# Scores of the latent attention as three rounded products instead of fp32 ones, high parts made by ScalarE and low parts by GpSimd

## The chip, the cores and the metric

One Trainium2 chip, one of its cores. The metric is the device time of one launch in microseconds. The kernel before was run three times: median 1334.41 us, from 1334.18 to 1334.98. The engines are called PE (TensorE), ACT (ScalarE), DVE (VectorE), POOL (GpSimd) and SP (SyncE); PEld is PE's weight load.

## The reference

A trunk of two layers runs over two requests of 256 tokens, 1024 channels, in float32. The even layer has, beside Mamba-2 heads (SSD), eight heads of multi-head latent attention (MLA); its part is

```
q = einsum('bsr,rf->bsf', rmsnorm(q_a, q_norm_w), w_qb)      # per head 128 "nope" + 64 "rope" columns
c_kv = rmsnorm(kv_a[..., :128], kv_norm_w)
q_rope, k_rope = apply_rope(q[..., 128:]), apply_rope(kv_a[..., 128:])
q_lat = einsum('bshd,chd->bshc', q_nope, w_uk)
sc = einsum('bqhc,bkc->bhqk', q_lat, c_kv) + einsum('bqhr,bkr->bhqk', q_rope, k_rope)
pr = softmax(sc * (128 + 64) ** -0.5)
o = (pr @ c_kv) @ w_uv
```

The concatenation of the SSD output and o goes through w_out, a norm and the residual; then come a convolutional FFN, a layer of gated linear attention (GLA) and another FFN. The scores `sc`, of 128 + 64 contracted rows per head, are what the change is about.

## The kernel before, in words

Everything is kept transposed: a tile has 128 channels as partitions and T = 512 columns, 2 requests of 256 tokens. The program has one instruction list for each engine, written out by hand, with semaphores between them; every engine works through its list in order. A weight block is loaded by SP (`load`, L294), rounded by ACT into `whi` (`hi`, L306) and the rest is taken by POOL into `wlo` (`lo`, L312, L316); `three` (L329 to L335) then makes a product of three rounded (fp32r) ones, whi x high, whi x low and wlo x high, without the product of the two low parts. Nearly all of PE's time is L333, L334 and L335. `his` and `los` (L319, L324) split the blocks that are due at a point. A slot for a block is free again when the products on it have incremented `mm_block`, on which SP waits.

The attention stage runs from about 198 to 283 us of the span, for 8 heads in 4 pairs; i is the pair, u the head in it, n = 2i + u the head. In `pe_mla` (L1425) a pair's queries (`queries`, L1432), keys (`keys`, L1442), values by token (`by_token`, L1455) and rope part (`rope`, L1472) are rounded products of weights and of the normed latents. ACT copies them out of PSUM (`copy`, L1570, to qh, kh, vp), DVE multiplies the rope product with cosines and sines into qre (`rope`, L1643), two 64-row halves for each head. `kre` (L1404), the rotated key part shared by all heads, is the sum of two parts. These are float32 tiles, and the scores (`scores`, L1491) are float32 products, which the profile shows as two instructions each (x2):

```
first = nc.tensor.matmul(o, qh[u][:, q], kh[u][:, keys_of], start=True, stop=False)      # L1502
last = nc.tensor.matmul(o, qre[u][:, q], kre[:, keys_of], start=False, stop=True)        # L1505
```

for 2 requests and 2 blocks of 128 queries against 256 keys. DVE then takes the maxima (`top`, L1657) and scales them (L1660), ACT takes the exponentials (`soft`, L1591) in four parts, DVE normalises (`norm`, L1666 and L1670), PE transposes (`turn`, L1519), ACT and DVE each copy a half into probT (`turned`, L1601 and L1678), PE multiplies with the values (`values`, L1532), and ACT and DVE make the high and low parts of the output, co_hi and co_lo (`outs`, L1605 and L1682).

PE's order in the stage: the parts of pair 0; then for each head n: scores(n), turn(n-1), parts of the next pair (queries and keys of its first head on even n, rope, queries and keys of its second head on odd n), values(n-1), by_token on even n. by_token(1) stands in turn 1. scores(n) waits for the copies, for qre and for the exponentials of head n-1, which free its PSUM banks.

ACT's order: copies of pair 0 around the square of the last SSD chunk (`act_ssd_square`, L1229) and one weight split, then for each n: its half of probT of n-1, soft(n), two copies of the next pair, rounded SSD chunks (`act_ssd_high`, L1267), the high part of the output of n-1, two value copies on even n, weight splits on even n. Two square roots with a table load stand in turn 0.

DVE's order for each n: top(n), its half of probT of n-1, on odd n the rope parts of the next pair with a product on zbuf between (`dve_ssd_norm`, L1262), norm(n), the low part of the output of n-1, low parts of SSD chunks (`dve_ssd_low`, L1272), two reciprocals of 128 columns in turns 1 to 4 (L1206).

POOL's list has the sum of squares of the SSD chunks (L1141), the last of which waits for ACT's last square, and then in this stage only weight splits (`pool_mla`, L1711). Behind the stage `pe_out` (L389) multiplies with w_out, the first product beside the last values and turn; the chunks of xw_hi and xw_lo, co_hi and co_lo are its operands.

Pieces of SBUF that are free in this stage: the last chunk of co_lo (chunk 7), chunks 6 and 7 of co_hi, xw_hi and xw_lo are written only in its last turns.

## Time and profile before

| what | value |
|---|---|
| median of 3 runs | 1334.41 us |
| the profiled execution | 1333.35 us |
| its span in the profile | 1331.5 us |
| PE busy | 1312.0 us (99%) |
| DVE busy | 772.5 us (58%) |
| ACT busy | 642.2 us (48%) |
| POOL busy | 620.4 us (47%) |
| mean granted clock of PE | 0.998 |

The profile is of one execution; times in its rows are microseconds from the start of its span. The time of the execution is 1.85 us longer than the span. In a timeline a row is: start, duration, engine, line, operation, output tile <- inputs, shapes, count, and in brackets the idle time of the engine before it with what ended it. Rows with x2 or more merge neighbours. A matmul's duration goes over into the next one's; the distance of starts is what it takes of PE.

### The profile page before, as it was taken

Reading aid. Unit: us, or ns where it says so; the run is one execution under the profiler, and the core shown is the slowest. Engines: PE = TensorE matmul, PEld = TensorE weight load, DVE = VectorE, ACT = ScalarE, POOL = GpSimd, SP = SyncE. Lnnn points to the kernel's source line nnn. Section 1 sums busy time; section 2 is a strip of 40 time slices with the busy share of each in tenths; the row PEclk is TensorE's granted clock in tenths of the full one; section 3 lists DMA queues with packets and bytes.
Section 4 is the critical chain, followed back from the end, with each engine's and each line's share of the span. In section 5 each row is a group of like instructions: output and inputs, shape, how many; then the busy total and the mean of one; then the engine's idle time right before and its main releaser. Section 6 shows DMA issues by size and latency. Waiting matters only on the chain.

```text
span 1331.5 us, 16312 instructions
## 1 busy us (share of the span) xinstructions
PE 1312.0 (99%) x6566; PEld 1110.9 (83%) x6566; DVE 772.5 (58%) x846; ACT 642.2 (48%) x1033; POOL 620.4 (47%) x294
## 2 busy tenths in 40 slices
PE   7999999999999999999999999999999999999997
PEld 6878878888898888888889988888998888888887
DVE  5857386840079998885001863546379988882002
ACT  6654787653355544444223486654555444443221
POOL 3344561245524554445454354654534554445551
PEclk9999999999999999999999999999999999999999
DMA  6342111123323333333332323311223333333331
GB/s 207 95 116 83 51 37 41 64 80 95 90 85 96 97 102 101 95 91 88 103 98 84 122 64 95 96 50 68 89 96 95 97 103 100 96 89 90 98 88 64
DMA packets 41451, 119.77 MB, mean 90 GB/s; under 512 B 4384, under 2 KB 12960, under 8 KB 41376
## 3 DMA queue, kind: packets, MB, share of 16 engines
q1 hardware_dynamic: 40160, 116.34, 28.3%
q10 hardware_dynamic: 1216, 2.38, 0.6%
q8 instruction: 52, 0.85, 0.3%
q14 instruction: 23, 0.19, 0.0%
HBM read 116.35 MB, written 2.23 MB: 89 GB/s over the span
## 4 chain that ended last, share of the span: by engine, by line
PE 93%; DVE 4%; ACT 1%; issue 1%; DMA 0%; ACTq 0%; DVEq 0%
PE bank L333 27%; PE bank L334 26%; PE bank L335 26%; PE bank L1771 1%; PE bank L1770 1%; PE bank L1769 1%; PE bank L2009 1%; PE bank L1502 1%; PE bank L1505 1%; PE bank L1322 1%; PE bank L384 1%; PE bank L1991 1%; PE bank L1289 1%; PE bank L1532 1%; DVE sqacc L660 1%
## 5 line engine op out<-in xcount | busy, mean ns | idle before, releaser
L316 POOL TENSOR_TENSOR wlo<-raw,whi 128x1024 fp32r<-128x1024 f32 (+2 forms) x215 | 528.6, 2472 | 630.7 <-ACT whi L310 630.6
L333 PE MATMUL bank<-xw_hi,whi 128*128 128x512 f32 (+1 forms) x1280 | 477.4, 373 | 8.6 <-DVE xw_lo L643 8.1
L335 PE MATMUL bank<-xw_hi,wlo 128*128 128x512 f32 (+1 forms) x1280 | 473.3, 370 | 0.0
L334 PE MATMUL bank<-xw_lo,whi 128*128 128x512 f32 (+1 forms) x1280 | 473.3, 370 | 0.0
L310 ACT ACTIVATE whi<-raw 128x1024 fp32r<-128x1024 f32 (+2 forms) x217 | 221.5, 1025 | 205.9 <-DMA raw<-in_fout 112.0
L333 PEld LDWEIGHTS bank<-xw_hi,whi 128*128 128x128 f32 x1280 | 242.0, 189 | 50.2 <-issue 8.9
L335 PEld LDWEIGHTS bank<-xw_hi,wlo 128*128 128x128 f32 x1280 | 241.9, 189 | 41.1
L334 PEld LDWEIGHTS bank<-xw_lo,whi 128*128 128x128 f32 x1280 | 242.0, 189 | 39.9 <-issue 0.2
L593 DVE RECIPROCAL small<-small 128x2 f32<-128x2 f32 x8 | 1.3, 166 | 315.1 <-ACT small L518 313.8
L712 DVE SCALAR_TENSOR_TENSOR cbuf<-ubuf,par,cbuf 128x510 f32<-128x510 f32 x100 | 168.8, 1688 | 3.5
L708 DVE SCALAR_TENSOR_TENSOR cbuf<-ubuf,par,cbuf 128x510 f32<-128x510 f32 x100 | 155.9, 1559 | 4.7 <-ACT cbuf L841 4.1
L333 PE MATMUL bank<-g_hi,whi 128*128 128x512 f32 (+1 forms) x396 | 145.3, 367 | 0.2
L335 PE MATMUL bank<-g_hi,wlo 128*128 128x512 f32 (+1 forms) x396 | 144.7, 365 | 0.0
L334 PE MATMUL bank<-g_lo,whi 128*128 128x512 f32 (+1 forms) x396 | 144.7, 365 | 0.0
L717 DVE TENSOR_TENSOR ubuf<-bank,rstd 128x512 f32<-128x512 f32 x116 | 78.0, 686 | 100.5 <-PE bank L335 91.1
L753 ACT ACTIVATE g_hi<-cbuf 128x512 fp32r<-128x512 f32 x44 | 27.8, 632 | 197.3 <-DVE cbuf L779 197.3
L333 PEld LDWEIGHTS bank<-g_hi,whi 128*128 128x128 f32 x396 | 74.7, 189 | 13.1 <-DVE g_lo L761 1.0
L334 PEld LDWEIGHTS bank<-g_lo,whi 128*128 128x128 f32 x396 | 74.7, 189 | 12.1
L335 PEld LDWEIGHTS bank<-g_hi,wlo 128*128 128x128 f32 x396 | 74.7, 189 | 11.9
L742 ACT ACTIVATE cbuf<-ubuf,par 128x512 f32<-128x512 f32 x88 | 69.9, 813 | 29.9 <-DVE ubuf L717 29.9
L779 DVE TENSOR_TENSOR cbuf<-cbuf 128x512 f32<-128x512 f32 x44 | 36.7, 834 | 1.5
L572 POOL TENSOR_TENSOR sqacc<-sqacc,cbuf 128x512 f32<-128x512 f32 x23 | 29.7, 1291 | 15.9 <-ACT cbuf L493 15.6
(275 smaller groups left out, 1435.5 us busy)
## 6 DMA issues: line engine op xcount, KB each, us to landing
raw<-in_fin SPq DMA_DIRECT2D x88, 512.0 KB, 3.6
raw<-in_fout SPq DMA_DIRECT2D x32, 448.0 KB, 3.3
raw<-in_gin SPq DMA_DIRECT2D x25, 512.0 KB, 3.6
raw<-in_hin SPq DMA_DIRECT2D x24, 512.0 KB, 3.6
raw<-in_hout SPq DMA_DIRECT2D x16, 512.0 KB, 3.7
raw<-in_fout SPq DMA_DIRECT2D x16, 512.0 KB, 3.6
raw<-in_gout SPq DMA_DIRECT2D x8, 512.0 KB, 3.7
xres<-in_x SPq DMA_DIRECT2D x8, 256.0 KB, 5.8
```

Source lines behind the costliest of these rows:

```text
L310: nc.scalar.activation(whi[s][:, 0:n], raw[s][:, 0:n], ACT.Copy).then_inc(w_hi, 1)
L316: engine.tensor_tensor(wlo[s][:, 0:n], raw[s][:, 0:n], whi[s][:, 0:n].bitcast(F32), ALU.subtract).then_inc(w_lo, 1)
L333: first = nc.tensor.matmul(out_ap, wh, ah, start=start, stop=False)
L334: nc.tensor.matmul(out_ap, wh, al, start=False, stop=False)
L335: return first, nc.tensor.matmul(out_ap, wl, ah, start=False, stop=stop)
L572: nc.gpsimd.tensor_tensor(sqacc[:], sqacc[:], cbuf[c % 2][:], ALU.add).then_inc(sem("out_acc"), 1)
L708: nc.vector.scalar_tensor_tensor(out=req(dst[:])[:, :, 1:SEQ], in0=req(src[:])[:, :, 0:SEQ - 1], scalar=prm(w, of), in1=req(dst[:])[:, :, ...
L712: nc.vector.scalar_tensor_tensor(out=req(dst[:])[:, :, 0:SEQ - 1], in0=req(src[:])[:, :, 1:SEQ], scalar=prm(w, of + 2 * n), in1=req(dst[:] ...
L717: return nc.vector.tensor_tensor(out_ap, src[:], rstd[:], ALU.mult)
L742: nc.scalar.activation(cbuf[u][:], ubuf[u][:], ACT.Identity, bias=prm(f"fb{l}", u * FF + t), scale=prm(f"fw{l}", 2 * FF + u * FF + t)).the ...
L753: nc.scalar.activation(ck(g_hi, t), cbuf[3][:], ACT.Copy).then_inc(sem("fin_hi"), 1)
L779: nc.vector.tensor_tensor(cbuf[3][:], cbuf[2][:], cbuf[1][:], ALU.mult).then_inc(sem("fin_prod"), 1)
```

## The change

The tiles qh, kh, qre and kre stay as float32 tiles; a rounded tile of the same size (qh_lo and so on) lies at the same address, so that the low part takes the place of the whole. The high parts go to the free chunks of co_lo, co_hi, xw_hi and xw_lo. ACT makes a high part of each with a copy (`high`, `rope_high`), POOL the low part as the difference (`low`), DVE that of kre. `scores` uses `rounded`, three products of 256 columns for each one before, and waits for POOL's low parts (`mla_xl`) instead of ACT's copies and DVE's rope. POOL's weight splits are put between its low parts, and ACT's copies of an odd turn alternate with the high parts of the ropes.

```diff
--- before.py
+++ after.py
@@ -111,6 +111,12 @@
         def sb(name, cols, dtype=F32, stack=ctx, parts=P):
             return stack.enter_context(nc.sbuf_tensor(name, [parts, cols], dtype))
 
+
+        def with_low(name, stack):
+
+            with ExitStack() as s:
+                whole = sb(name, T, F32, s)
+            return whole, sb(name + "_lo", T, F32R, stack)
 
         xres = sb("xres", KD * T)
         raw, wlo, whi = [], [], []
@@ -176,11 +182,12 @@
                 qn_lo = sb("qn_lo", 2 * T, F32R, q)
                 ckv_hi = sb("ckv_hi", T, F32R, q)
                 ckv_lo = sb("ckv_lo", T, F32R, q)
-                kre = sb("kre", T, F32, q)
-                qre1 = sb("qre1", T, F32, q)
-                qh = [sb(f"qh{i}", T, F32, q) for i in range(2)]
-                qre = [sb("qre0", T, F32, q), qre1]
-                kh = [sb(f"kh{i}", T, F32, q) for i in range(2)]
+                kre, kre_lo = with_low("kre", q)
+                (qre1, qre1_lo) = with_low("qre1", q)
+                qh, qh_lo = zip(*(with_low(f"qh{i}", q) for i in range(2)))
+                qre0, qre0_lo = with_low("qre0", q)
+                qre, qre_lo = [qre0, qre1], [qre0_lo, qre1_lo]
+                kh, kh_lo = zip(*(with_low(f"kh{i}", q) for i in range(2)))
                 vp0 = sb("vp0", NBLK * 2 * P, F32, q)
                 prob0 = sb("prob0", 4 * SEQ, F32, q)
                 probT = sb("probT", 4 * SEQ, F32, q)
@@ -1403,12 +1410,21 @@
             dve.wait_ge(sem("ssd_y"), 16)
             nc.vector.tensor_tensor(kre[:], kr_part[0][:], kr_part[1][:], ALU.add).then_inc(sem("mla_kd"), 1)
 
+        kre_hi = ck(co_lo, 7)
+        qre_hi = [ck(co_hi, 6 + u) for u in range(2)]
+        qh_hi = [ck(xw_hi, 6 + u) for u in range(2)]
+        kh_hi = [ck(xw_lo, 6 + u) for u in range(2)]
+
         MLA_FIRST = ("rope", "q0", "k0", "v0", "v1", "q1", "k1")
         MLA_PARTS = ("q0", "k0", "v0", "v1", "rope", "q1", "k1")
 
         def mla_part(i, part):
 
             return 7 * i + (MLA_PARTS if i else MLA_FIRST).index(part) + 1
+
+        def split(i, part):
+
+            return 6 * i + ("q0", "k0", "r0", "r1", "q1", "k1").index(part) + 1
 
         def rope_bank(i):
 
@@ -1488,10 +1504,15 @@
                 queries(i, 1)
                 keys(i, 1)
 
+            def rounded(o, a, b, keys_of, q, start, stop):
+
+                first = nc.tensor.matmul(o, a[0][:, q], b[0][:, keys_of], start=start, stop=False)
+                nc.tensor.matmul(o, a[0][:, q], b[1][:, keys_of], start=False, stop=False)
+                return first, nc.tensor.matmul(o, a[1][:, q], b[0][:, keys_of], start=False, stop=stop)
+
             def scores(n):
                 i, u = n // 2, n % 2
-                pe.wait_ge(sem("mla_act"), made(i, 6 if u else 2))
-                pe.wait_ge(sem("mla_qr"), 4 * i + 2 * u + 2)
+                pe.wait_ge(sem("mla_xl"), split(i, "k1" if u else "r0"))
                 if n:
                     pe.wait_ge(sem("mla_exp"), 4 * n)
                 for r in range(NREQ):
@@ -1499,10 +1520,10 @@
                     for qb in range(2):
                         o = bank[2 + r][:, qb * SEQ:(qb + 1) * SEQ]
                         q = slice(r * SEQ + qb * P, r * SEQ + (qb + 1) * P)
-                        first = nc.tensor.matmul(o, qh[u][:, q], kh[u][:, keys_of], start=True, stop=False)
+                        first, _ = rounded(o, (qh_hi[u], qh_lo[u]), (kh_hi[u], kh_lo[u]), keys_of, q, True, False)
                         if n == 0 and r == 0 and qb == 0:
                             first.then_inc(mm, 1)
-                        last = nc.tensor.matmul(o, qre[u][:, q], kre[:, keys_of], start=False, stop=True)
+                        _, last = rounded(o, (qre_hi[u], qre_lo[u]), (kre_hi, kre_lo), keys_of, q, False, True)
                     last.then_inc(sem("mla_s"), 1)
 
             def turn(n):
@@ -1540,7 +1561,7 @@
             by_token(0)
             queries(0, 1)
             keys(0, 1)
-            pe.wait_ge(sem("mla_kd"), 3)
+            pe.wait_ge(sem("mla_kd"), 5)
             for n in range(MHEADS):
                 more = n // 2 + 1 < MHEADS // 2
                 scores(n)
@@ -1582,6 +1603,17 @@
                 src = (bank[0], k_bank(i, 0), bank[0], bank[v_bank(i, 1)], bank[1], k_bank(i, 1))[e]
                 nc.scalar.activation(out_ap, src[:], ACT.Copy).then_inc(sem("mla_act"), 1)
 
+            def rope_high(i, u):
+
+                act.wait_ge(sem("mla_qr"), 4 * i + 2 * u + 2)
+                nc.scalar.activation(qre_hi[u], qre[u][:], ACT.Copy).then_inc(sem("mla_xh"), 1)
+
+            def high(i, u):
+
+                for j, (hi_of, src) in enumerate(((qh_hi, qh), (kh_hi, kh))):
+                    act.wait_ge(sem("mla_act"), 6 * i + 4 * u + j + 1)
+                    nc.scalar.activation(hi_of[u], src[u][:], ACT.Copy).then_inc(sem("mla_xh"), 1)
+
             def soft(n):
                 u = n % 2
                 act.wait_ge(sem("mla_nm"), n + 1)
@@ -1605,12 +1637,18 @@
                 nc.scalar.activation(ck(co_hi, n), bank[6 + n % 2][:], ACT.Copy).then_inc(sem("mla_ohi"), 1)
             for e in range(2):
                 copy(0, e)
+            high(0, 0)
             act_ssd_square(act, KD - 1)
+            rope_high(0, 0)
+            act.wait_ge(sem("mla_kd"), 3)
+            nc.scalar.activation(kre_hi, kre[:], ACT.Copy).then_inc(sem("mla_kd"), 1)
             for e in (2, 3):
                 copy(0, e)
+            rope_high(0, 1)
             his(act, base)
             for e in (4, 5):
                 copy(0, e)
+            high(0, 1)
             nc.scalar.activation(small[:, 5:6], prm("eps"), ACT.Exp)
             for n in range(MHEADS):
                 more = n // 2 + 1 < MHEADS // 2
@@ -1621,8 +1659,15 @@
                         copy(1, e)
                 soft(n)
                 if more:
-                    for e in ((4, 5) if n % 2 else (0, 1)):
-                        copy(n // 2 + 1, e)
+                    if n % 2:
+                        rope_high(n // 2 + 1, 0)
+                        copy(n // 2 + 1, 4)
+                        rope_high(n // 2 + 1, 1)
+                        copy(n // 2 + 1, 5)
+                    else:
+                        for e in range(2):
+                            copy(n // 2 + 1, e)
+                    high(n // 2 + 1, n % 2)
                 for c in beside(n):
                     act_ssd_high(act, c)
                 if n:
@@ -1684,6 +1729,8 @@
             rope(0, 0)
             dve_mla_prep(dve)
             rope(0, 1)
+            dve.wait_ge(sem("mla_kd"), 4)
+            nc.vector.tensor_tensor(kre_lo[:], kre[:], kre_hi.bitcast(F32), ALU.subtract).then_inc(sem("mla_kd"), 1)
             for n in range(MHEADS):
                 more = n % 2 and n // 2 + 1 < MHEADS // 2
                 top(n)
@@ -1709,8 +1756,28 @@
             outs(MHEADS - 1)
 
         def pool_mla(pool):
-            for i in range(8):
-                los(pool, BASE["mla"] + i)
+            base = BASE["mla"]
+
+            def low(i, part):
+
+                low_of, src, high = {"q": (qh_lo, qh, qh_hi), "k": (kh_lo, kh, kh_hi), "r": (qre_lo, qre, qre_hi)}[part[0]]
+                u = int(part[1])
+                pool.wait_ge(sem("mla_xh"), split(i, part))
+                nc.gpsimd.tensor_tensor(low_of[u][:], src[u][:], high[u].bitcast(F32),
+                                        ALU.subtract).then_inc(sem("mla_xl"), 1)
+            for part in ("q0", "k0", "r0", "r1"):
+                low(0, part)
+            los(pool, base)
+            for part in ("q1", "k1"):
+                low(0, part)
+            for i in range(1, MHEADS // 2):
+                for part in ("q0", "k0"):
+                    low(i, part)
+                for at in (2 * i - 1, 2 * i):
+                    los(pool, base + at)
+                for part in ("r0", "r1", "q1", "k1"):
+                    low(i, part)
+            los(pool, base + 7)
 
 
 
```

## Rows read from the trace of the kernel before

**Rows 1.** The page, part 4: the chain that ended last, by engine.
```profile
PE 93%; DVE 4%; ACT 1%; issue 1%; DMA 0%; ACTq 0%; DVEq 0%
```

**Rows 2.** Windows of the stage: PE, PEld, DVE, ACT, POOL busy us (instructions), clock, DMA.
```profile
198.00:209.00 11.00, 10.97 (x53) 9.18 (x54) 6.51 (x11) 6.01 (x10) 2.58 (x2) 1.00 0.20 61
209.00:219.00 10.00, 9.90 (x52) 7.95 (x51) 5.82 (x8) 8.80 (x19) 2.83 (x2) 1.00 0.00 1
...
252.00:271.00 19.00, 18.43 (x92) 15.63 (x91) 17.45 (x28) 13.06 (x31) 4.83 (x3) 1.00 0.17 56
```

**Rows 3.** PE timeline: start, duration; scores of head 5 begin, and what follows begins.
```profile
251.79 0.60 PE L1502 MATMUL bank<-kh,qh 128*128 128x256 f32 x2
...
255.25 1.04 PE L1519 MATMUL bank<-ident,prob 128*128 128x128 f32 x8
```

**Rows 4.** PE timeline: first and last of seven neighbouring rounded products of 256 columns.
```profile
202.04 0.28 PE L1469 MATMUL bank<-wlo,ckv_hi 128*128 128x256 f32 x1
...
202.75 0.28 PE L1469 MATMUL bank<-wlo,ckv_hi 128*128 128x256 f32 x1
```

**Rows 5.** PE timeline: first rounded products behind the transposes of head 2.
```profile
236.99 0.47 PE L333 MATMUL bank<-qn_hi,whi 128*128 128x512 f32 x1
237.30 0.40 PE L334 MATMUL bank<-qn_lo,whi 128*128 128x512 f32 x1
```

**Rows 6.** ACT and DVE timelines before the first scores.
```profile
201.72 0.60 ACT L1583 ACTIVATE kh<-bank 128x512 f32<-128x512 f32 x1
202.22 0.62 ACT L1233 ACTIVATE sqbuf<-zbuf 128x512 f32<-128x512 f32 x1
...
201.85 0.69 DVE L1404 TENSOR_TENSOR kre<-kr_part 128x512 f32<-128x512 f32 x1
```

**Rows 7.** POOL timeline around the first scores.
```profile
202.92 1.30 POOL L1141 TENSOR_TENSOR sqacc<-sqacc,sqbuf 128x512 f32<-128x512 f32 x1 [6.88 <-ACT sqbuf L1233]
204.62 1.28 POOL L316 TENSOR_TENSOR wlo<-raw,whi 128x512 fp32r<-128x512 f32 x1 [0.40 <-ACT whi L310]
```

**Rows 8.** PE timeline: scores 0 and 1 begin, rope product of pair 1, scores 2.
```profile
205.29 0.59 PE L1502 MATMUL bank<-kh,qh 128*128 128x256 f32 x2
...
211.96 0.67 PE L1502 MATMUL bank<-kh,qh 128*128 128x256 f32 x2
...
217.92 0.50 PE L333 MATMUL bank<-qn_hi,whi 128*128 128x512 f32 x1
...
223.19 0.59 PE L1502 MATMUL bank<-kh,qh 128*128 128x256 f32 x2
```

**Rows 9.** POOL and DVE timelines from 216; then L1660's durations, min/median/max.
```profile
216.18 3.09 POOL L316 TENSOR_TENSOR wlo<-raw,whi 128x768 fp32r<-128x768 f32 x2 [10.28 <-ACT whi L310]
...
216.41 1.63 DVE L1660 TENSOR_SCALAR stat<-stat 128x4 f32<-128x4 f32 x1
...
L1660 DVE TENSOR_SCALAR stat<-stat x8: 170/171/1632, 209.7 to 272.8; 128x4 f32<-128x4 f32 x8
```

**Rows 10.** DVE, PE and ACT timelines: rope of head 4, its scores, output of head 2.
```profile
238.66 1.40 DVE L1650 TENSOR_TENSOR qre<-bank,cosin 64x512 f32<-64x512 f32 x2 [0.66 <-PE bank L335]
...
242.24 0.59 PE L1502 MATMUL bank<-kh,qh 128*128 128x256 f32 x2
...
242.44 0.60 ACT L1605 ACTIVATE co_hi<-bank 128x512 fp32r<-128x512 f32 x1 [0.52 <-PE bank L1532]
```

**Rows 11.** PE timeline: values of head 5, and the first output product on co_hi.
```profile
266.12 1.97 PE L1532 MATMUL bank<-probT,vp 128*128 128x256 f32 x8 [0.34 <-ACT probT L1601]
...
283.25 0.39 PE L333 MATMUL bank<-co_hi,whi 128*128 128x512 f32 x1
```

**Rows 12.** PE timeline at the kernel's start.
```profile
8.11 0.55 PE L333 MATMUL bank<-xw_hi,whi 128*128 128x256 f32 x1 [8.11 <-DVE xw_lo L643]
8.46 0.42 PE L334 MATMUL bank<-xw_lo,whi 128*128 128x256 f32 x1
...
11.24 0.36 PE L335 MATMUL bank<-xw_hi,wlo 128*128 128x256 f32 x1
```

## The prediction

> **What bounds the kernel now.** I read the page first: TensorE (PE) holds 93% of the chain that ended last [rows 1]. The windows, next, show the same inside the attention stage: PE busy 10.97 of 11.0 us from 198 to 209 and 18.43 of 19.0 from 252 to 271, while POOL is idle for three quarters of it; ACT and DVE have stretches with hardly a pause (8.80 of 10, 17.45 of 19) [rows 2]. So a shorter product pays in full, if what feeds it stays in time; and the timelines of the other queues must be read for how much time they have in hand.
>
> **What PE gains.** One head's scores are 16 fp32 instructions of 256 columns (each product is two of them), from 251.79 to 255.25: 3.46 us, 0.216 each [rows 3]. Afterwards they are 24 rounded ones. The same shape exists already, whi times ckv: six between 202.04 and 202.75 stand 0.119 apart [rows 4]. 24 x 0.119 = 2.86 us, so 0.60 less per head and 4.8 for 8 heads. The first rounded product behind fp32 ones takes longer (236.99 to 237.30, 0.31 instead of 0.23 [rows 5]); the scores of four heads now follow fp32 products: 4 x 0.08 = 0.3. Gain 4.5 us. The Trainium skill (TensorE: Matmul & The Clock Gate, Back-to-back issue gap) gives N/2.4 + 2.5 ns between starts, 109 ns at 256 columns. By it the gain, as an estimate, would be 6.7 us; the trace's 0.119 is used.
>
> **What is added.** ACT: for each of the 4 pairs of heads six high copies (q0, k0, r0, r1, q1, k1), and one of kre, 25 in all, each 128x512. Such an instruction takes 0.60, and neighbours start 0.50 apart (201.72 to 202.22 [rows 6]): 12.5 us of ACT. POOL: 24 subtractions of 512 columns, 1.28 us like the 512-wide weight split [rows 7]; in a row I take 1.24, from the 3.09 of a pair with 1280 columns [rows 9]: 30 us. DVE: one subtraction, 0.69 like kre's own addition [rows 6]. No DMA is added or moved, but POOL's and ACT's weight splits are now queued among these. The splits still end before PE wants them (keys of pair 1: by 212.0, wanted near 214.7), and SP's loads are released by PE's own products and move with it: both at nothing. Nor would the rest cost PE a thing were it always in time. It isn't, and I walk the queues in order, each instruction with its own row's length.
>
> *First scores.* Before, they start at 205.29, right behind the key product [rows 8]. ACT copies q0, then k0 at 201.72, and squares at 202.22 [rows 6]. Two high copies now stand ahead of that square (+1.0), so it ends near 203.8. POOL's sum of squares waits for the square (before: 202.92, 1.30 us [rows 7]) and stands ahead of all low parts; it now ends near 205.1. Three subtractions (q0, k0, r0) of 1.24 give 208.8, and DVE's kre_lo (0.69), with two inputs in SBUF, takes as much of POOL's time (below). PE starts at about 209.5: **+4.2**. The cover that is gone is only 0.2 us wide, so nothing hides this. ACT's other additions there (rope_high, kre_hi, 1.0 us ahead of the first value copy) delay the keys of head 1 by about 0.9, inside the same hole.
>
> *DVE against POOL.* While POOL ran its split from 216.18, DVE's 128x4 scaling of the maxima took 1.63 us, against a median of 0.17 [rows 9]. It ended when POOL's instruction did. So such a DVE instruction waits for POOL's, and the other way round. The Trainium skill (SBUF — State Buffer, SBUF: two separate sides) says that the two share a port pair as an exclusive lock, for DVE in a two-port mode or with two SBUF inputs; by that rule the normalisation of the probabilities, the zbuf products and the low parts of xw are caught too. The trace agrees for the scaling; of the others every instance in this stage fell beside an idle POOL. I charge them all, up to 1.24 us for each collision, as the one row at 1.63 has it.
>
> *Scores 1 and 2.* From scores 0, PE is 0.6 shorter, but the scaling of head 0 meets POOL's queue (r1, a split, q1, k1 without pause until 214.5): +1.1. Scores 1, which wait for ACT's four exponentials: 216.6 against 211.96, **+4.6**. ACT is busy 8.80 of 10 us from 209 to 219 [rows 2], so the two high copies there go straight into its queue (+1.0); rope 1 waits for ACT's value copy: 223.3 against 217.92, and scores 2 come at 228.7 against 223.19, **+5.5**, just behind r0's subtraction.
>
> *Steady part.* Scores 3 and 4 stay at +5.5: PE's 0.6 per head is lost to by_token waiting for copies (0.4) and to r0. The r0 chain is the tight one: PE's rope product, DVE 1.40, ACT 0.6, POOL 1.28. For head 4 it begins at 238.66 on DVE and PE wants scores at 242.24 [rows 10]: 3.6 us for 3.3 us of work, and a lock on top.
> The second loop is ACT's order. On an odd turn two rope copies, the second waiting for DVE, and two high copies stand ahead of the output copy (before at 242.44, 0.2 behind the start of scores [rows 10]); it now comes 2.6 us behind it. DVE's low part of the output waits for it, in order, and behind it stand reciprocals or low parts of xw, then the maxima, the scaling and probT. Before, DVE was busy 17.45 of the 19 us from 252 [rows 2], and the values of head 5 waited 0.34 already [rows 11]. So delay there reaches PE in full: scores 5 **+7**, scores 6 (r0 of pair 3 late by 1.7) **+8**, scores 7 (two low parts of xw behind POOL, values 3.8 late) **+11**. The last head adds 0.5: the output products, at 283.25 before [rows 11], come some **11 us** later. The walk without the change, with the same rules, puts them within 0.2 us of 283.25.
> Behind the stage PE is bound by itself again and weights are ahead; the shift stays. The sum holds the gain of 4.5 already, so the waits come to some 15.5 us.
>
> Bounds. Low end: POOL 1.20, ACT 0.45 per copy and no lock, +7. High end: ACT 0.60 per copy (its unpipelined length) with the lock, +13. I take 11, nearer the high end, for the 1.63 row. Profiled execution: 1333.35 + 11 = 1344.4; the median is 1.1 above it: **1345.4 us**.
>
> **Rivals.**
> A. The lock catches only the small scaling: then the walk gives about +8, 1342.4. For it: only that instruction was seen blocked here. 0.15.
> B. Only the first wait shows, and later ones vanish in slack I have missed (ACT passes 5 us more of idle than I read, or copies finish sooner): 4.2 - 4.5, that is 1334.1. For it: POOL is mostly idle [rows 2]. Against: the in-order queues, where the idle time lies in front of PE's results and not behind them. 0.11.
> C. Faster. If POOL's first three low parts come by 206.9 instead of 209.5 (were the sum of squares not in the way and the subtraction nearer ACT's 0.5), and later ones in time, PE's products decide: 4.5 gained, 1.6 lost, 1331.5. It decides from a first wait under 1.8 us. Against: POOL's rows leave no such speed. 0.09.
> D. The clock. After PE's idle 8.1 us at the kernel's start its rounded 256-column products stood 0.214 apart (14 starts from 8.46 to 11.24 [rows 12]), where rows 4 have 0.119: some 1.4 us lost, a spacing that fits the lower of its two levels (1.2 and 2.4 GHz), though the granted clock reads 1.00 there. The hole of 3.4 to 3.6 us before scores 0 may do the same: scores 0 then 2.2 us longer; part of it is hidden by ACT. 1347 to 1349. Against: no row shows how long a hole it takes, and the clock reads 1.00 through this stage [rows 2]. 0.15. The Trainium skill (TensorE: Matmul & The Clock Gate, HAM oscillation) warns that waits between bursts throw the engine back to half clock; the start of this trace agrees, for the middle no row here shows it.
> That the change does not do what it says (fp32 products kept) is excluded by its text: the operands are rounded tiles of the type that rows 4 show.
>
> **How the numbers follow.** Forecast (+9.5 to +13) 0.50, A 0.15, D 0.15, B 0.11, C 0.09. A measurement of this kernel can tell about 0.2%, 2.7 us. Faster: most of C, 0.08. Within: B and the rest of C, 0.12. Slower: 0.80. The range takes in the forecast, A and D, and some smaller-than-A outcomes: 1338 to 1350.
>
> **What would show it.** Right: scores' products 0.119 apart; a PE hole of 3 us or more before scores 0 with POOL's k0 and r0 subtractions inside it; scaling instructions of over 1 us; values of head 5 waiting for DVE's probT; the stage ending 11 us late and nothing changed after it. Wrong: scores 0 before 208; scores 3 to 5 less than 3 us late (slack missed, B); a granted clock of 0.5 in the stage (D); scaling at 0.17 throughout and no long normalisation (A).

## The result and the profile after

The change makes the kernel **slower**, by 0.8%: 1344.67 us (median of 4 runs, 1344.31 to 1344.93) against 1334.30 (1333.86 to 1334.98) on the same chip, a ratio of 1.0081 with a 95% interval of 1.007 to 1.0093. Forecast were 1345.4 us and a range of 1338 to 1350. The profiled execution took 1344.31 us.

The page of the changed kernel: its span, part 1, and the first line of part 4 (the chain that ended last, by engine).

```profile
span 1342.5 us, 16490 instructions
...
PE 1312.4 (98%) x6630; PEld 1112.9 (83%) x6630; DVE 772.0 (58%) x847; ACT 653.5 (49%) x1058; POOL 654.1 (49%) x318
...
PE 90%; DVE 4%; ACT 3%; issue 1%; POOL 1%; DMA 1%; DVEq 0%; ACTq 0%
```

PE's share of the chain fell from 93% [rows 1] to 90%; ACT's rose from 1% to 3%, and POOL is on it for the first time. ACT is busy 11.3 us more and POOL 33.7 us more than in the table of before, while PE's busy time is 0.4 us above the old value, although its products need some 4 us less (experiment 1): a slower clock has lengthened some of them, as will be seen.

The waits of PE in the stretch from 195 to 290 us (the attention stage): tile and line that waited, what it waited for, us in total, times, longest.

```profile
PE bank L1509 <- POOL qre_lo L1766: 4.3, 3, 3.1
PE bank L1553 <- DVE probT L1723: 4.0, 2, 3.2
PE bank L340 <- ACT vp L1604: 2.0, 2, 1.3
...
PE bank L1483 <- ACT qh L1604: 0.7, 1, 0.7
...
PE bank L1553 <- DVE co_lo L1727: 0.3, 1, 0.3
PE bank L1509 <- ACT prob L1623: 0.3, 1, 0.3
```

These six make 11.6 us; the kernel before has 0.9 us of waits in its stage (a product on xw_lo 0.4, values 0.3, scores 0.2). Waits that both kernels have ahead of the attention (1.7 and 0.4 us) are left out. The windows of the changed kernel, with the columns of [rows 2]:

```profile
199.00:210.00 11.00, 7.43 (x36) 5.41 (x35) 6.33 (x10) 8.15 (x16) 5.34 (x4) 1.00 0.13 38
209.00:219.00 10.00, 8.64 (x44) 7.51 (x45) 2.76 (x5) 5.33 (x15) 6.04 (x5) 0.83 0.10 30
252.00:271.00 19.00, 16.37 (x99) 13.93 (x98) 16.22 (x26) 13.63 (x33) 10.57 (x8) 1.00 0.18 56
271.00:285.00 14.00, 10.15 (x65) 9.06 (x64) 10.73 (x17) 7.74 (x19) 6.64 (x4) 0.88 0.01 3
```

Where [rows 2] have PE at 10.97 of 11 and 18.43 of 19, PE now idles 3.6 us in the window ahead of the first scores, 2.6 us in the third window and 3.9 us in the fourth. The granted clock, 1.00 throughout before, is 0.83 and 0.88 in two of the four. The PE timeline at the first of the two places:

```profile
206.73 0.40 PE L342 MATMUL bank<-ckv_hi,wlo 128*128 128x512 f32 x1
210.23 0.36 PE L1509 MATMUL bank<-xw_lo,xw_hi 128*128 128x256 f32 x1 [3.11 <-POOL qre_lo L1766]
...
210.54 0.28 PE L1511 MATMUL bank<-xw_lo,qh_lo 128*128 128x256 f32 x1
210.66 0.28 PE L1509 MATMUL bank<-co_lo,co_hi 128*128 128x256 f32 x1
...
212.00 0.41 PE L1511 MATMUL bank<-co_lo,qre_lo 128*128 128x256 f32 x1
212.21 0.41 PE L1509 MATMUL bank<-xw_lo,xw_hi 128*128 128x256 f32 x1
```

The products start 0.12 apart at first (210.54, 210.66), as in [rows 4], and from 211.14 to 214.55 they are 0.213 apart (212.00, 212.21): of the two levels of the clock that is the lower, 1.2 GHz. Sixteen distances lengthened by 0.094 cost 1.5 us. The same at the second place, in the scores of head 7:

```profile
280.34 0.41 PE L1511 MATMUL bank<-xw_lo,qh_lo 128*128 128x256 f32 x1
280.55 0.41 PE L1509 MATMUL bank<-co_lo,co_hi 128*128 128x256 f32 x1
```

These scores take 4.28 us (279.77 to 284.05), against 2.94 for the undisturbed ones of head 1.

For a comparison by stage I take the start of the scores of each head, counted from the first rope product of the stage (198.02 before, 198.74 after; the 0.72 between them arises ahead of the attention, and differs from profile to profile: 197.8 to 199.1 over all profiles of this study). "Forecast" is what the prediction gave.

| start of | before | after | delay | forecast |
|---|---|---|---|---|
| scores 0 | 7.27 | 11.49 | +4.2 | +4.2 |
| scores 1 | 13.94 | 19.13 | +5.2 | +4.6 |
| scores 2 | 25.17 | 31.45 | +6.3 | +5.5 |
| scores 3 | 34.72 | 40.86 | +6.1 | +5.5 |
| scores 4 | 44.22 | 49.67 | +5.5 | +5.5 |
| scores 5 | 53.77 | 60.82 | +7.1 | +7 |
| scores 6 | 63.27 | 70.95 | +7.7 | +8 |
| scores 7 | 70.29 | 81.03 | +10.7 | +11 |
| first product on co_hi | 85.23 | 96.10 | +10.9 | +11 |

Behind the stage the shift stays: the spans differ by 11.0 us.

### The profile page after: what moved, and what is told of

It reads as the page before. It is cut to its first block, busy times and chain, and to the rows that moved or that the text cites. A ratio compares the mean times of both kernels' runs of the same rounds, so it can differ in the third digit from the quotient of the medians.

```text
span 1342.5 us, 16490 instructions
## 1 busy us (share of the span) xinstructions
PE 1312.4 (98%) x6630; PEld 1112.9 (83%) x6630; DVE 772.0 (58%) x847; ACT 653.5 (49%) x1058; POOL 654.1 (49%) x318
## 4 chain that ended last, share of the span: by engine, by line
PE 90%; DVE 4%; ACT 3%; issue 1%; POOL 1%; DMA 1%; DVEq 0%; ACTq 0%
PE bank L340 26%; PE bank L341 26%; PE bank L342 26%; PE bank L1838 1%; PE bank L1836 1%; PE bank L1837 1%; PE bank L2076 1%; PE bank L391 1%; PE bank L1329 1%; PE bank L1296 1%; PE bank L2058 1%; ACT prob L1623 1%; DVE cbuf L715 1%; PE bank L1298 1%; DVE cbuf L719 0%
## 5 line engine op out<-in xcount | busy, mean ns | idle before, releaser
L719 DVE SCALAR_TENSOR_TENSOR cbuf<-ubuf,par,cbuf 128x510 f32<-128x510 f32 x100 | 168.8, 1688 | 3.5
L715 DVE SCALAR_TENSOR_TENSOR cbuf<-ubuf,par,cbuf 128x510 f32<-128x510 f32 x100 | 151.4, 1514 | 4.7 <-ACT cbuf L848 4.1
L760 ACT ACTIVATE g_hi<-cbuf 128x512 fp32r<-128x512 f32 x44 | 27.8, 632 | 197.0 <-DVE cbuf L786 197.0
L786 DVE TENSOR_TENSOR cbuf<-cbuf 128x512 f32<-128x512 f32 x44 | 40.8, 928 | 1.5
```

Source lines behind the costliest of these rows:

```text
L715: nc.vector.scalar_tensor_tensor(out=req(dst[:])[:, :, 1:SEQ], in0=req(src[:])[:, :, 0:SEQ - 1], scalar=prm(w, of), in1=req(dst[:])[:, :, ...
L719: nc.vector.scalar_tensor_tensor(out=req(dst[:])[:, :, 0:SEQ - 1], in0=req(src[:])[:, :, 1:SEQ], scalar=prm(w, of + 2 * n), in1=req(dst[:] ...
L760: nc.scalar.activation(ck(g_hi, t), cbuf[3][:], ACT.Copy).then_inc(sem("fin_hi"), 1)
L786: nc.vector.tensor_tensor(cbuf[3][:], cbuf[2][:], cbuf[1][:], ALU.mult).then_inc(sem("fin_prod"), 1)
```

## Experiments

All ratios are to the kernel before, run on the same chip in the same batch; its medians were 1333.69, 1333.53 and 1333.92 us in the three batches, so a version that costs what the change costs would read 1343.9 to 1344.7. "At co_hi" is the first product on co_hi, counted as in the table.

### 1. The products alone

The scores' three products read operands that exist anyway, and none of the high and low parts is made. Left out: the attention scores themselves.

```diff
-                        first, _ = rounded(o, (qh_hi[u], qh_lo[u]), (kh_hi[u], kh_lo[u]), keys_of, q, True, False)
+                        first, _ = rounded(o, (qn_hi, qn_lo), (ckv_hi, ckv_lo), keys_of, q, True, False)
...
-                        _, last = rounded(o, (qre_hi[u], qre_lo[u]), (kre_hi, kre_lo), keys_of, q, False, True)
+                        _, last = rounded(o, (qn_hi, qn_lo), (ckv_hi, ckv_lo), keys_of, q, False, True)
...
-                pe.wait_ge(sem("mla_xl"), split(i, "k1" if u else "r0"))
+                pe.wait_ge(sem("mla_act"), made(i, 6 if u else 2))
+                pe.wait_ge(sem("mla_qr"), 4 * i + 2 * u + 2)
```

> Only PE's side of the change: scores are 24 rounded products of 256 columns per head, on tiles that exist anyway (qn and ckv, high and low), with the waits of the kernel before; no high or low parts of queries, keys and ropes are made. It leaves out the true scores. The sum of the prediction for PE alone says 4.5 us less than before: 1329.8. The walk of the queues says that the chain through DVE and ACT in heads 5 to 7 gives half of that back: 2 less, 1332.2. If the three products were no cheaper on PE than the two fp32 ones, 1334.3.

Measured: 1331.08 us (10 runs, 1330.35 to 1331.72), ratio 0.998 [0.9971, 0.9989]. The scores come 0.6 us earlier at head 1, 3.2 us at head 6, but only 2.5 us at heads 7 and at co_hi. PE's waits in the stage say why:

```profile
PE bank L1554 <- DVE probT L1719: 1.0, 2, 0.7
```

Nothing was added here, so the wait comes from DVE's own list, which has no room for a PE that is 3 us ahead: DVE was busy 17.45 of 19 us from 252 [rows 2]. The products themselves gain 4.1 us and not 4.5: over the eight heads the scores take 23.7 us in place of 27.8. Of that, 2.5 us (0.2%) reach co_hi, so this is the most that the change could have won with the lists of ACT and DVE as they are.

### 2. High parts without low parts

ACT makes all high parts, DVE still subtracts for kre, POOL makes no low part; the scores multiply high parts three times. Left out: the low parts of queries, keys and ropes.

```diff
-                pe.wait_ge(sem("mla_xl"), split(i, "k1" if u else "r0"))
+                pe.wait_ge(sem("mla_xh"), split(i, "k1" if u else "r0"))
...
-                pool.wait_ge(sem("mla_xh"), split(i, part))
-                nc.gpsimd.tensor_tensor(low_of[u][:], src[u][:], high[u].bitcast(F32),
-                                        ALU.subtract).then_inc(sem("mla_xl"), 1)
+                return
```

> The change without POOL's 24 low parts: scores wait for ACT's high parts and take a high part wherever the low one stood, so the second and third product of each score are wrong; all of PE's, ACT's and DVE's work is kept. Walk: 6 us over the kernel before, 1340.3, so POOL's subtractions and what they do to DVE would be worth 4.5 us and ACT's copies 8. If POOL's low parts carried nearly all of the loss, below 1335. No hole of over 3 us before the first scores, so a granted clock of 1.0 there.

Measured: 1338.87 us (4 runs, 1338.36 to 1339.62), ratio 1.0042 [1.0027, 1.0057]; +5.1 at co_hi. With the two neighbours that parts the account of the change: from products alone (-2.5) to high parts (+5.1) ACT's copies cost 7.6 us, and from there to the change (+10.9) POOL's low parts cost 5.8. Of these, 3.2 fall before the first scores (7.27 before, 8.26 with high parts, 11.49 with both), and 1.5 are the dip of the clock behind them, which this kernel doesn't have there (scores 0 take 2.88 us here and 4.44 in the change). Some 1.1 us are left for everything else that the low parts do. That is an estimate, since the clock falls once here too, at the end of the wait of 2.4 us below, and scores 7 take 3.85 us, so that the 7.6 hold a part of a dip. PE's waits of this kernel in the stage:

```profile
PE bank L1553 <- DVE probT L1723: 3.2, 2, 2.4
PE bank L340 <- ACT vp L1604: 2.0, 2, 1.3
...
PE bank L1553 <- ACT probT L1633: 1.3, 1, 1.3
PE bank L1483 <- ACT qh L1604: 1.2, 2, 0.7
```

The wait for probT stands here without any work of POOL. It is the order of ACT's list that makes it.

### 3. ACT's copy of the output first

In each turn the copy that makes co_hi goes ahead of the high parts of the next pair (and of the second rope part). The work is that of the change.

```diff
                         rope_high(n // 2 + 1, 0)
                         copy(n // 2 + 1, 4)
-                        rope_high(n // 2 + 1, 1)
                         copy(n // 2 + 1, 5)
...
-                    high(n // 2 + 1, n % 2)
...
                     for e in (2, 3):
                         copy(n // 2 + 1, e)
+                if more:
+                    if n % 2:
+                        rope_high(n // 2 + 1, 1)
+                    high(n // 2 + 1, n % 2)
```

> The change with ACT's order altered alone: on odd turns the output's high part goes ahead of the second rope copy and the two high copies, on even turns ahead of the high copies. If the second loop (ACT's late output, DVE's low part, maxima, probT, values) costs what the walk says, 2.7 us less than the change: 1342.0, with the values of heads 3 and 5 waiting less than 2 us for DVE's probT. If low parts are what matters, they come later by this order and the time rises to 1345 or more.

Measured: 1341.64 us (1341.34 to 1341.9), ratio 1.0063 [1.0046, 1.0079]; 2.7 us less at co_hi than the change. In the change ACT's and DVE's timelines show the chain for head 5 (start, duration; ACT, then DVE):

```profile
272.66 0.58 ACT L1637 ACTIVATE co_hi<-bank 128x512 fp32r<-128x512 f32 x1
...
273.28 0.69 DVE L1727 TENSOR_TENSOR co_lo<-bank,co_hi 128x512 fp32r<-128x512 f32 x1 [1.85 <-ACT co_hi L1637]
273.89 2.37 DVE L1281 SCALAR_TENSOR_TENSOR xw_lo<-zbuf,par,xw_hi 128x512 fp32r<-128x512 f32 x2
276.18 1.28 DVE L1702 TENSOR_REDUCE stat<-bank 128x2 f32<-128x512 f32 x2
277.49 0.17 DVE L1705 TENSOR_SCALAR stat<-stat 128x4 f32<-128x4 f32 x1
277.57 0.69 DVE L1723 COPY probT<-bank 128x512 f32<-128x512 f32 x1
```

DVE idles 1.85 us for co_hi, and what stands behind in its list (xw_lo, the maxima, scaling) puts the copy into probT at 277.57, for which PE waits 3.19 us at 278.32. With the output copy first DVE's co_lo starts at 270.07 without a wait, and PE's waits read:

```profile
PE bank L1509 <- POOL qre_lo L1768: 5.4, 3, 3.1
PE bank L340 <- ACT vp L1604: 2.0, 2, 1.3
...
PE bank L1553 <- DVE probT L1725: 0.5, 2, 0.3
```

The wait for probT went from 4.0 to 0.5 us; 1.1 us of the 3.5 came back as a longer wait for qre_lo, because PE reaches scores 6 that much sooner than the low part does: PE is 2.1 us earlier at scores 5, DVE's rope for pair 3 only 1.1, as it stands behind a scaling of the maxima that POOL held up for 2.1 us (last section). So the theory held, price included.

### 4. Pair 0 in fp32

The scores of heads 0 and 1 stay as before; the high and low parts of pair 0 and of kre are not made at the stage's start (kre's are made in turns 0 and 1).

```diff
-                pe.wait_ge(sem("mla_xl"), split(i, "k1" if u else "r0"))
+                if i:
+                    pe.wait_ge(sem("mla_xl"), split(i, "k1" if u else "r0"))
+                else:
+                    pe.wait_ge(sem("mla_act"), made(i, 6 if u else 2))
+                    pe.wait_ge(sem("mla_qr"), 2 * u + 2)
...
+                        if i == 0:
+                            first = nc.tensor.matmul(o, qh[u][:, q], kh[u][:, keys_of], start=True, stop=False)
...
+                            last = nc.tensor.matmul(o, qre[u][:, q], kre[:, keys_of], start=False, stop=True)
+                            continue
```

> The change with heads 0 and 1 left as fp32 products: no high and low parts for pair 0, the two parts of kre made later (high in ACT's turn 0, low in DVE's turn 1, kept beside kre). The first scores then start where they did before, 7.3 us after the stage's first product, and the first clock dip is gone. Walk: 4.5 us less than the change for the whole stage, 1340. If the first wait were taken up by slack in later turns, the gain would be under 1.5 us: 1343 or more.

Measured: 1339.91 us (1339.29 to 1340.26), ratio 1.005 [1.0035, 1.0065]; +6.4 at co_hi, 4.5 less than the change. Scores 0 and 1 start as before (7.30, 13.96). The first hole of 3.1 us and the first clock dip are gone; the wait of 3.2 us for probT stands unaltered. Scores 1 come 5.2 us earlier than in the change, scores 2 to 7 4.6 to 4.7, and the difference is the 0.6 that the scores of head 1 take longer in fp32. So the first wait is passed on in full and later waits absorb none of it: the next ones are not made by an engine that had been ahead, but by chains that begin with PE's own products and move with it.

### 5. Pair 3 in fp32

As above for heads 6 and 7, whose queries and keys are made in turns 4 and 5, beside three of the normalised SSD chunks; pair 2 meets one (`i == 3` in place of `i == 0`).

> The change with heads 6 and 7 left as fp32 products, pairs 0 to 2 rounded; all else in place. Walk: 4.1 us less than the change (1340.5), of which 2.6 would go even without any collision of POOL and DVE, and 1.5 is DVE's low parts of xw held by POOL's subtractions. If pair 3's low parts cost nothing and only the product form matters, it gets slower by the 1.1 us that PE would save there.

Measured: 1340.22 us (1339.74 to 1341.04), ratio 1.0053 [1.0038, 1.0068]; 3.9 us less than the change at co_hi, all of it in the last two heads (scores 5 at 60.88 against 60.82, scores 7 at 77.27 against 81.03). PE's wait for probT is 0.8, and the second dip of the clock isn't there. How much of it is DVE held by POOL, 1.5 us by the expectation, this run doesn't separate.

### 6. Both early edits together

Pair 0 in fp32 and the output copy first, the edits of 4 and 3.

> Both edits at once: the scores of heads 0 and 1 as before, in fp32, and ACT's copy of the attention output ahead of the high parts. Each alone gave back time: 4.5 us at the first output product for the first, 2.7 us for the second. Theory (the first wait and the order of ACT's list are two costs that lie one after the other on PE's path): they add, the output products come 3.7 us behind the kernel before and the time is 1337.5, at most 1338.5; PE's wait for DVE's probT is under 1 us. Rival (both edits give back the same waits of heads 5 to 7, which only need everything to be earlier): no more than the larger of the two comes back, 1339.5 to 1340.

Measured: 1337.40 us (9 runs, 1336.01 to 1337.59), ratio 1.0025 [1.0015, 1.0035]. At co_hi 7.0 us less than the change; the two alone gave 4.5 + 2.7 = 7.2. They add, the rival is out. One part of the expectation failed: PE still waits 1.7 us for DVE's probT, in the values of head 5, where under 1 us was expected, and the clock falls behind that wait.

### 7. Only pairs 1 and 2, output copy first

The three edits 3, 4 and 5 together: four heads of eight use rounded products.

> Only heads 2 to 5 rounded (pairs 1 and 2), and ACT's order with the output first. Walk: 0.6 us over the kernel before, 1334.5: the costs at both ends are gone, PE saves 2.2 us in the middle and loses as much to ACT's longer turn 0 (rope product of pair 1 later by 1.4) and to DVE. If the waits in the middle are as dear as at the ends, 1338 or more; if they are hidden, 1332.

Measured: 1333.80 us (10 runs, 1332.99 to 1334.67), ratio 1.0004 [0.9994, 1.0013]; scores 7 at 70.43, co_hi at 85.37, both 0.1 us behind the kernel before. It costs nothing and wins nothing: four heads give 2 us of PE time, and one wait of 1.2 us for vp (rope of pair 1) and the tight DVE list take it. No version of the study is faster than the kernel before and still computes the same.

### 8. Eleven idle products in the hole

Does the dip of the clock cost anything? PE multiplies, in the hole before scores 0, into a bank that nobody reads.

```diff
+            for k in range(11):
+                nc.tensor.matmul(bank[7][:], ckv_hi[:, 0:P], ckv_hi[:], start=k == 0, stop=k == 10)
             pe.wait_ge(sem("mla_kd"), 5)
```

> The change with 11 products of 512 columns on an unused bank put into PE's hole before the first scores (2.5 us of idle time filled), nothing else. If the clock fell there because PE stood idle, it stays at 1.0 through scores 0, these end 1.6 us earlier, and the time is 1343.1; if the dip comes whatever PE does, or what follows waits for something else anyway, 1344.7.

Measured: 1343.99 us (1342.76 to 1344.11), ratio 1.0077 [1.0062, 1.0092], between the two forecasts, and too near the change for the medians to tell them apart; in the two profiles co_hi comes 0.7 us sooner. PE's timeline:

```profile
206.07 2.69 PE L1565 MATMUL bank<-ckv_hi 128*128 128x512 f32 x11
209.42 0.36 PE L1509 MATMUL bank<-xw_lo,xw_hi 128*128 128x256 f32 x1 [0.66 <-POOL qre_lo L1768]
...
212.12 0.28 PE L1510 MATMUL bank<-kre_lo,co_hi 128*128 128x256 f32 x1
212.25 0.28 PE L1511 MATMUL bank<-co_lo,qre_lo 128*128 128x256 f32 x1
212.37 1.02 PE L1572 MATMUL bank<-sqacc,ones 128*128 128x512 f32 x2
...
216.40 0.36 PE L1509 MATMUL bank<-xw_lo,xw_hi 128*128 128x256 f32 x1 [0.94 <-ACT prob L1625]
```

The dip is gone: scores 0 take 2.95 us (209.42 to 212.37) in place of 4.44 (210.23 to 214.67). But scores 1 then wait 0.94. POOL's and DVE's timelines name the cause:

```profile
212.95 1.31 POOL L1768 TENSOR_TENSOR kh_lo<-kh,xw_lo 128x512 fp32r<-128x512 f32 x1
...
213.29 0.99 DVE L1707 TENSOR_SCALAR stat<-stat 128x4 f32<-128x4 f32 x1
```

The scaling of the maxima, counted from the stage's start 1.4 us earlier than in the change, falls under POOL's last subtraction and is held to its end (212.95 + 1.31 = 214.26; 213.29 + 0.99 = 214.28). In the change scores 0 were so slow that it met an idle POOL. So the one cost hid the other: take the dip away (scores 0 end 1.4 us sooner) and the held scaling takes its place, so that scores 1 come only 0.55 us sooner.

### 9. POOL's work beside the old kernel

The kernel before with as many subtractions of 512 columns on POOL at the same places of its list; nobody uses their results, and ACT, PE and DVE have their lists of before.

```diff
+            def beside(i, part):
...
+                    pool.wait_ge(sem("mla_act"), 6 * i + 4 * u + (1 if part[0] == "q" else 2))
+                nc.gpsimd.tensor_tensor(ck(co_lo, 7), ck(qn_hi, 0).bitcast(F32), ckv_hi[:].bitcast(F32),
+                                        ALU.subtract).then_inc(sem("pool_beside"), 1)
```

> The kernel before with 24 subtractions of 128x512 on POOL that nobody waits for until the stage's last output, at about the times of the change's low parts (their result is not used). If POOL's instructions exclude DVE's scaling and DVE's instructions with two SBUF inputs, both ways, as the prediction charged: 6.6 us over before, 1340.5. If they hold the scaling alone, about 2 us over; if they do not meet DVE at all, 1334.

Measured: 1341.16 us (1340.12 to 1341.67), ratio 1.0059 [1.0044, 1.0074]. Work that PE never waits for costs 7.6 us by the medians and 6.15 at co_hi, counted within the stage (in this profile the stage also starts 1.1 us later than in that of before). A dip of the clock has a part in the 6.15, beside a wait of 2.8 us for probT in the values of head 5: the granted clock is 0.88 from 266 to 280 us, the second half of these values takes 1.87 us (0.79 in experiment 1) and the scores of head 7 3.93 in place of 3.53, about 1.4 us more of PE's time. The groups of DVE by line in this kernel (durations in ns: min/median/max):

```profile
L1660 DVE TENSOR_SCALAR stat<-stat x8: 170/355/2082, 210.8 to 280.6; 128x4 f32<-128x4 f32 x8
...
L1670 DVE TENSOR_TENSOR prob<-prob,stat x8: 1224/1332/2252, 214.1 to 283.0; 128x1024 f32<-128x1024 f32 x8
...
L1274 DVE SCALAR_TENSOR_TENSOR xw_lo<-zbuf,par,xw_hi x8: 741/745/1747, 255.8 to 287.1; 128x512 fp32r<-128x512 f32 x8
...
L1682 DVE TENSOR_TENSOR co_lo<-bank,co_hi x7: 691/692/692, 227.0 to 284.5; 128x512 fp32r<-128x512 f32 x7
...
L1657 DVE TENSOR_REDUCE stat<-bank x16: 624/680/692, 208.3 to 279.9; 128x2 f32<-128x512 f32 x16
...
L1206 DVE RECIPROCAL rstd<-rstd x4: 895/919/942, 227.6 to 235.7; 128x128 f32<-128x128 f32 x4
```

The scaling, the normalisation and the low parts of xw are held, up to 1.9 us over their own 0.17, and 1.0 over 1.22 and 0.74. The instructions that read PSUM (co_lo, the maxima) and the reciprocals keep their time, although five of the co_lo, ten of the maxima and all of the reciprocals shown ran beside a POOL instruction. So not only the small scaling is caught: rival A falls. In the Trainium skill (SBUF — State Buffer, SBUF: two separate sides) the lock takes a DVE instruction "with two SBUF inputs (only against a GpSimd op that reads SBUF)" or in a two-port mode. The held and the free rows above agree with it, as far as they go: the scaling has one input, and whether it runs in such a mode no row shows.

### 10. POOL's low parts in halves

```diff
-                nc.gpsimd.tensor_tensor(low_of[u][:], src[u][:], high[u].bitcast(F32),
-                                        ALU.subtract).then_inc(sem("mla_xl"), 1)
+                for half in range(2):
+                    c = slice(half * SEQ, (half + 1) * SEQ)
+                    op = nc.gpsimd.tensor_tensor(low_of[u][:, c], src[u][:, c], high[u][:, c].bitcast(F32),
+                                                 ALU.subtract)
+                op.then_inc(sem("mla_xl"), 1)
```

> The change with each of POOL's low parts as two instructions of 256 columns in place of one of 512; nothing else is different. Theory (a DVE instruction that meets one of POOL's waits until that instruction is over): what DVE waits is halved at each collision, and scores 7 come about 1 us earlier: 1343.2, with POOL's instructions near 0.64 us and DVE's scaling never above 0.8 us. If a POOL instruction has a fixed part of 0.1 us or more, the first scores come 0.3 to 0.5 us later and the time stays at 1344. Rival (the lock weighs nothing in the sum, POOL's own length decides): 1344.2 or more, however the collisions go.

Measured: 1345.60 us (1345.04 to 1345.84), ratio 1.0088 [1.0071, 1.0105]: a miss for 1343.2; the interval takes in the change's own ratio, and the rival's 1344.2 or more is what came. At co_hi it is 1.8 us behind the change. POOL's groups show two instructions of 256 columns:

```profile
L1768 POOL TENSOR_TENSOR kh_lo<-kh,xw_lo x16: 718/739/1171, 207.2 to 276.7; 128x256 fp32r<-128x256 f32 x16
```

Two of them take 1.48, against 1.28 for one of 512: a fixed part of near 0.2 us, the case that the expectation put at 1344. DVE's scaling is still held once, to 0.91 us, where 0.8 was expected at most. Scores 0 come 0.46 later, the hole grows to 3.53, and the clock dip behind it covers all of scores 0 (products 0.213 apart to 215.13): +1.3 at scores 1, +2.4 at scores 2. Between scores 2 and scores 7 0.8 us of it come back. Whether that is the shorter lock can't be told from this run, because too much else moved; nothing in it speaks for a lock that weighs much in the sum.

## Why the prediction was right, point by point

**PE's gain.** Right in size: in experiment 1 the scores of head 0, behind other rounded products, take 2.87 us (205.75 to 208.62) where [rows 3] have 3.46, so 0.59; the forecast was 0.60. Over all heads it is 4.1 and not 4.5: heads 2, 4 and 6, whose scores follow fp32 products, take 3.06 us, 0.18 more each, where the prediction took off 0.08 for each of four heads. What the prediction didn't say is that alone this gain would bring only 2.5 us: from scores 6 on DVE's list takes the rest.

**First scores, +4.2.** Right to 0.1 us, and in its steps. POOL's timeline in the change:

```profile
204.66 1.29 POOL L1148 TENSOR_TENSOR sqacc<-sqacc,sqbuf 128x512 f32<-128x512 f32 x1 [7.90 <-ACT sqbuf L1240]
205.91 1.73 POOL L1766 TENSOR_TENSOR qh_lo<-qh,xw_hi 128x512 fp32r<-128x512 f32 x1
207.60 1.26 POOL L1766 TENSOR_TENSOR kh_lo<-kh,xw_lo 128x512 fp32r<-128x512 f32 x1
208.82 2.50 POOL L1766 TENSOR_TENSOR qre_lo<-qre,co_hi 128x512 fp32r<-128x512 f32 x2
```

Sum of squares first, then three subtractions, the first lengthened by 0.45 (the prediction charged 0.69) while DVE made kre_lo, and r0 at 210.1, when PE starts. The row of x2 counts r0 and r1.

**Scores 1, +4.6, measured +5.2.** The step that failed is the scaling held for 1.1 us: all eight took 0.17 to 0.20. Its place was taken by the dip of the clock, 1.5 us, that is by rival D. Experiment 8 shows both halves: without the dip the scaling is held 0.8 us. That the sum still came near is luck here: the prediction had the wrong cost at this place. The further +1.1 up to scores 2 is ACT's value copy, as forecast with +0.9 (PE waits 1.32 for vp; in [rows 8] the rope product has no wait).

**The lock.** It catches what the prediction charged, the normalisation and the low parts of xw too, and POOL in turn. The trace of before had a row against rival A, 3 us ahead of the stage, that the prediction passed over: one of two equal instructions took twice as long, beside POOL's sum of squares from 194.78 to 196.04.

```profile
L1386 DVE SCALAR_TENSOR_TENSOR qn_lo<-mq,par,qn_hi x2: 740/1120/1500, 195.1 to 196.5; 128x512 fp32r<-128x512 f32 x2
```

The longest of DVE's in the change, by line, and POOL's:

```profile
L1715 DVE TENSOR_TENSOR prob<-prob,stat x8: 1224/1225/1833, 218.0 to 287.4; 128x1024 f32<-128x1024 f32 x8
...
L1281 DVE SCALAR_TENSOR_TENSOR xw_lo<-zbuf,par,xw_hi x8: 741/746/1708, 261.9 to 291.4; 128x512 fp32r<-128x512 f32 x8
...
L1766 POOL TENSOR_TENSOR qre_lo<-qre,co_hi x8: 1261/1314/2273, 208.8 to 270.7; 128x512 fp32r<-128x512 f32 x8
```

Before, the longest of the first two groups took 1226 and 748 ns. But the prediction made the lock too dear. Its walk is 3 us shorter without it (rival A). In the change, behind the first scores, DVE is held three times and not at the scaling: the normalisation by 0.6 us, a product on zbuf by 0.25 and a low part of xw by 1.0. Only the last stands in the chain of head 5 that is shown in experiment 3, and experiment 2 leaves 1.1 us for all that the low parts do beside the first wait and the dip.

**Second loop, +7, +8, +11.** Right in size and in cause. The step "ACT's output copy is late, DVE waits, in order, then maxima, scaling, probT, values" is shown by experiments 2 and 3: it stands without POOL's work, and goes from 4.0 to 0.5 us when the copy goes first. That r0 of pair 3 (the low part of the first rope half that scores 6 need) is late shows as 1.07 us of wait at scores 6. The jump of 3 us between scores 6 and 7 is the 3.19 us wait for probT.

**Rivals.** B (slack) falls: experiment 4 gives back the whole first wait. C falls with POOL's rows. D happened, twice, and the prediction had left it out of its 11 us. That the total is right to 0.1 us is therefore luck in part: the first dip (1.5 us) stands where the held scaling was charged, and the lock was charged higher than the change shows it. The second dip lengthens the first product and 12 distances of scores 7, 1.3 us in all. Most of it is hidden: from scores 7 to co_hi the change takes 15.07 us, and experiment 3, with the same work there and no dip, takes 14.91, because its faster PE waits 0.3 us for probT and 0.4 for xw_lo; with a dip there experiments 4 and 6 take 15.2 to 15.3. So of the 1.3 us some 0.2 reach co_hi in the change, 0.3 in experiments 4 and 6.

**Its own signs.** The spacing of 0.119, the hole before scores 0 with POOL's k0 and r0 inside it, the wait for probT in the values of head 5 and the 11 us all came. The scaling of over 1 us did not, and two signs that it gave for being wrong were seen: a granted clock of 0.5 inside the stage (D), and the scaling near 0.17 throughout, though with a long normalisation beside it (A).

**The account.** Waits of PE in the stage 11.6 us, less 0.9 before; the two dips 1.5 + 1.3; PE's gain -4.1: 9.4 us. Measured are 10.9. The missing 1.5 would fit the starts behind a wait, where PE loses more than the bracket says: from 206.73 to 210.23 are 3.50 us, of which one product is 0.23 and the wait 3.11, so 0.16 is left, and the first product then takes 0.19 in place of 0.12. The new waits are ten against three before; seven times 0.23 is 1.6. That is an estimate, not shown. The prediction's 15.5 us of waits (11 + 4.5) have 15.0 against them (10.9 + 4.1), of which waits proper are 10.7.

## What to carry to other kernels

When an engine at 99% gets less to do, the gain is worth only what its feeders can follow; try the shorter product with operands that exist already before building what it needs (here 2.5 us of a forecast 4.5), and compare that ceiling with the price of the feeders. Added work on a half idle engine isn't free if it stands in an in-order list ahead of something that a third engine waits for: the copy of the output behind four high parts cost 2.7 us and could be undone by order alone. And in these traces a POOL instruction of 1.3 to 2.4 us held DVE instructions that take both inputs from SBUF, and a scaling of four columns besides, which stood on the path; so where both engines are used, look at the largest duration of each DVE group and not at its mean.

## What the runs showed that I had not expected

- The clock fell in mid-kernel after PE had been idle, and came back while it worked. In the change both long holes (3.11 us before scores 0, 3.19 us in the values of head 5) are followed by a stretch at the lower of the two levels, 211.14 to 214.55 behind the first. In experiment 3 a wait of 2.07 us ahead of scores 6 was followed by one as well, but the same wait of 2.07 in experiment 6 was not, and one of 1.72 us some 7 us later was; the waits of 1.3 us for vp were followed by none in any run. So the length of a hole alone doesn't decide, and what does these runs don't show. Behind the 3.53 us hole of experiment 10 the lower clock covered all of scores 0: the window from 209 to 219 reads 0.66, where the change reads 0.83. The Trainium skill (TensorE: Matmul & The Clock Gate, HAM oscillation) tells of such throttling between bursts; the trace agrees.
- A DVE instruction of four columns took 2.26 us in experiment 3, where its own time is 0.17, because it began beside a weight split of 1024 columns:

```profile
262.02 2.26 DVE L1707 TENSOR_SCALAR stat<-stat 128x4 f32<-128x4 f32 x1
```

- POOL's work alone, used by nobody, costs this kernel 6.15 us in the stage (experiment 9), more than half of the change's 10.9, a part of it by a dip of the clock. It doesn't simply add to the rest: in the change the low parts cost 5.8 us over the high parts, of which 3.2 are plain lateness at the first scores and 1.5 the dip behind it.
- One cost can mask another, as the dip did with the scaling's hold: 1.5 us taken away gave 0.7 at co_hi.
